# A mixture of experts in float32: the second layer in four column chunks, the spread by row groups, and each further pass in a condition of its own

## The reference

```python
logits = xt @ w_router + b_router                 # 256 x 32
top_v, top_e = lax.top_k(logits, 4)
weights = jax.nn.softmax(top_v, axis=-1)
# for each expert e and its tokens:
hcat = x @ w1[e] + b1[e]                          # 1024 -> 2048
x_glu = minimum(hcat[:, ::2], 7.0)
x_lin = clip(hcat[:, 1::2], -7.0, 7.0)
act = x_glu * sigmoid(1.702 * x_glu) * (x_lin + 1.0)
y = act @ w2[e] + b2[e]                           # 1024 -> 1024
# out[token] = sum over its 4 experts of weight * y
```

## Time and profile before

| | before |
|---|---|
| median of 3 runs | 2322.46 us (2321.23 to 2323.91) |
| the profiled execution, its own time | 2310.58 us |
| its span, first to last instruction | 2308.8 us |
| busy PE, DVE, ACT, POOL | 80%, 35%, 22%, 3% |
| moved by DMA | 713.56 MB |
| the first mixture's experts, in the span | from 427.6 to about 1460 us |

### The profile page before, as it was taken

How to read it: one execution, slowest core, us unless ns; L and a number is a source line. 1 busy time by engine, 2 the same in 40 slices (tenths; PEclk the granted TensorE clock), 3 DMA queues, 4 the chain that set the end, 5 groups by cost and what they waited for, 6 DMA issues and landing times. The chain is left out here.

```text
span 2308.8 us, 28283 instructions
## 1 busy us (share of the span) xinstructions
PE 1839.7 (80%) x11518; PEld 837.9 (36%) x11518; DVE 811.2 (35%) x1618; ACT 496.6 (22%) x1005; POOL 76.8 (3%) x96
## 2 busy tenths in 40 slices
PE   7899998888989988789977788689968656555555
PEld 3655545433333333333333333354524422222221
DVE  2224332333433334433344334687682300000001
ACT  2032301222222133332333333321301200000000
POOL 0000000000000000000000000291000000000000
PEclk9999999899999999999999999799989777777778
DMA  8745268498797699999999999432126399999996
GB/s 287 268 146 181 93 215 310 176 398 329 328 388 318 278 424 408 422 424 376 406 423 423 423 417 420 143 117 103 40 73 236 122 426 428 428 427 427 425 424 260
DMA packets 113956, 713.56 MB, mean 309 GB/s; under 512 B 16703, under 2 KB 21006, under 8 KB 68654
## 3 DMA queue, kind: packets, MB, share of 16 engines
q1 hardware_dynamic: 105344, 704.98, 75.3%
q10 hardware_dynamic: 8398, 5.47, 0.8%
HBM read 709.35 MB, written 1.07 MB: 308 GB/s over the span
## 5 line engine op out<-in xcount | busy, mean ns | idle before, releaser
L779 PE MATMUL ps<-ring,ar 128*32 128x512 f32 x3072 | 374.5, 627 | 50.2 <-DMA ring<-in_w 21.7
L434 PE MATMUL ps<-ar 128*128 128x128 f32 (+5 forms) x1750 | 357.9, 361 | 41.9 <-PEq L691 13.4
L441 PE MATMUL ps<-ring,ar 128*32 128x512 f32 x1536 | 211.5, 713 | 192.1 <-DMA ring<-in_w_up 81.0
L434 PEld LDWEIGHTS ps<-ar 128*128 128x128 f32 (+2 forms) x1750 | 235.9, 201 | 165.8 <-issue 111.1
L434 PE MATMUL ps<-ring,ar 128*128 128x512 f32 (+2 forms) x624 | 262.9, 581 | 18.0 <-DVE ar L1855 9.9
L779 PEld LDWEIGHTS ps<-ring,ar 128*32 128x32 f32 x3072 | 99.8, 113 | 318.9 <-issue 275.8
L1610 DVE TENSOR_SCALAR ar<-ps 128x256 f32<-128x256 f32 x128 | 54.4, 425 | 432.2 <-PE ps L779 425.5
L790 PE MATMUL ps<-ring,ar 128*32 128x512 f32 x1536 | 175.2, 595 | 21.7 <-ACT ar L2207 21.7
L441 PEld LDWEIGHTS ps<-ring,ar 128*32 128x32 f32 x1536 | 60.6, 129 | 337.0 <-issue 336.1
L434 PEld LDWEIGHTS ps<-ring,ar 128*128 128x128 f32 x624 | 119.2, 193 | 156.4 <-issue 135.6
L538 PE MATMUL ps<-ring,ar 128*128 128x512 f32 x384 | 172.4, 598 | 3.4 <-ACT ar L2038 3.4
(11 more groups left out here) (393 smaller groups left out, 1290.5 us busy)
## 6 DMA issues: line engine op xcount, KB each, us to landing
ring<-in_w SPq DMA_DIRECT2D x192, 2048.0 KB, 18.4
ring<-in_w_gate SPq DMA_DIRECT2D x32, 2048.0 KB, 17.8
ring<-in_w_up SPq DMA_DIRECT2D x32, 2048.0 KB, 16.8
ring<-in_w_down SPq DMA_DIRECT2D x32, 2048.0 KB, 16.3
ring<-in_w_in SPq DMA_DIRECT2D x21, 2048.0 KB, 8.1
ring<-in_w_ada SPq DMA_DIRECT2D x12, 2048.0 KB, 8.6
ring<-in_w_out SPq DMA_DIRECT2D x4, 2048.0 KB, 8.1
ring<-in_w_branch SPq DMA_DIRECT2D x6, 1024.0 KB, 5.0
```

The lines of the kernel that those rows point to most:

```text
L434: ins = self.t.e.matmul(o, l, r, start=(i == 0), stop=(i == len(pairs) - 1))
L441: ins = self.t.e.matmul(b[32 * i:32 * i + 32, :], l, r, start=(k == 0), stop=(k == len(steps) - 1))
L779: ins = e.matmul(b[32 * s:32 * s + 32, :], HG[:, 2 * c + r, 32 * n:32 * n + 32], W[:, r, HALF(s)], start=False, stop=(c == 3 and r == 1))
```

## The change

Layer two: each pass has 32 matmuls of 256 columns instead of 16 of 512. Column group `c` holds result columns 256c to 256c+255 and sums the whole contraction. ACT evicts a pass in one instruction of 128x256. Spread: the stationary operand is now one row group (32 rows) of `SWT1`, the moving one 256 columns of `YG1`; 8 matmuls for each pass go side by side through four row groups into four banks. DVE then does four additions of 128x512 for each expert, in all cases. It stands between the halves of layer one. Conditions: each further pass has its own, in the order 3, 2, 1; the last of them counts on semaphores of its own (`s_px`, `s_py`, `s_ps`), and the Else no longer waits for `s_pe`. The count of expert `u + 1` is loaded once, in the second half of layer one. `turn_act(0)` moves into the middle of the next gather, and `turn_act(1)` runs always, before layer two. DVE does the spread's additions ahead of pass 0. `AT1` and `SB1` have one buffer instead of two.

```diff
+    def only(t, count, limit, body):
+        n, met = t.n, dict(t.met)
+        with t.e.If(count > limit):
+            body()
+        assert t.n == n
+        t.met = met
+
+    def either(t, x, count, limit, body):
+        n, m, met = t.n, x.n, dict(t.met)
+        with t.e.If(count > limit):
+            body()
+        assert t.n == n
+        t.met = met
+        with t.e.Else():
+            if m > 0:
+                t.e.wait_ge(x.sem, m)
+            t.e.nop().then_inc(x.sem, x.n - m)
...
+        def gather1(u, count, between):
+            pe["sw1", u, 0] = t(weights_turned(u, 0, (4,)))
+            rows_in(u, 0, (5,))
+            between()
+            only(t, count, 64, lambda: weights_turned(u, 2, (6,)))
+            rows_in(u, 1, (4,))
...
+        def spread1(u, count):
+            b = [w.claim("sp", u, c, lane=(SP1[c],)) for c in range(4)]
+            def rows(n, tb, first, last):
+                for c in range(4):
+                    r = slice(32 * c, 32 * c + 32)
+                    ins = e.matmul(b[c][:, 256 * tb:256 * tb + 256], SWT1[u % 2][r, n, TB(tb)], YG1[r, n, :],
+                                   start=first, stop=last)
+                return ins
+            t.wait_ge(s_act, act["yg", u, 0])
+            with e.If(count > 32):
+                for tb in range(2):
+                    t.wait_ge(s_act, act["yg", u, 1])
+                    rows(1, tb, True, False)
+                    def later():
+                        t.wait_ge(s_act, act["yg", u, 3])
+                        rows(2, tb, False, False)
+                        rows(3, tb, False, False)
+                    only(t, count, 64, later)
+                    ins = rows(0, tb, False, True)
+                z(ins)
+            with e.Else():
+                for tb in range(2):
+                    ins = rows(0, tb, True, True)
+                ins.then_inc(s_ps, z.n - n)
...
-            def layer2(b, n, arrive):
+            def layer2(b, n, arrive, first):
...
-                    for h in range(2):
-                        for r in range(2):
-                            ins = e.matmul(b[64 * h + 32 * r:64 * h + 32 * r + 32, :],
-                                           AT_[:, 2 * s + r, 32 * n:32 * n + 32], W[:, s % 2, r, HALF(h)],
-                                           start=(s == 0), stop=(s == 3))
+                    for r in range(2):
+                        for c in range(4):
+                            ins = e.matmul(b[32 * c:32 * c + 32, 0:256], AT1[:, 2 * s + r, 32 * n:32 * n + 32],
+                                           W[:, s % 2, r, 256 * c:256 * c + 256], start=(s == 0 and r == 0),
+                                           stop=(s == 3 and r == 1))
...
+                only(t, count, 96, lambda: further(3))
+                only(t, count, 64, lambda: further(2))
+                either(t, x, count, 32, lambda: x(further(1)))
...
+                if half == 0 and u > 0:
+                    spread1(u - 1, counts[u - 1])
...
-            if u > 0:
-                spread(t, w, 1, u - 1, TL1)
-            turn_act(0, (0,))
             if u + 1 < NE:
-                gather(t, w, 1, u + 1, TL1)
+                gather1(u + 1, counts[u + 1], turn_first)
+            else:
+                turn_first()
+            turn_act(1, (1,), (5,))
...
+            only(t, count, 64, lambda: turn_act(2, (2, 3), (6,)))
...
+            either(t, x, count, 32, second)
+            px["l2", u] = x.n
+            only(t, count, 96, fourth)
+            either(t, y, count, 64, third)
...
 vector_moe1
+            if u > 0:
+                vector_spread1(v, u - 1)
             for n in range(4):
-                M = TM[n % 2]
+                M = TM1[n % 2]
...
-                if n == 0 and u > 0:
-                    vector_spread(v, 1, u - 1)
...
 scalar_moe1
         for u in range(NE):
             sigmoid(u, 0)
+                weights_turned(u + 1, 0)
+            sigmoid(u, 1)
+                rows_in(u + 1, 0)
+            turned_act(u, 0, (0,))
+                weights_turned(u + 1, 2)
+                rows_in(u + 1, 1)
+            turned_act(u, 1, (1,))
+            sigmoid(u, 2)
+            sigmoid(u, 3)
+            evict(u, 0)
+            turned_act(u, 2, (2, 3))
             for n in (1, 2, 3):
+                evict(u, n)
```

More of the change, by code:

```diff
@@ L761, in tensor_moe1, with weights_turned, rows_in @@
         t.wait_ge(s_b1, 16)
-        gather(t, w, 1, 0, TL1)
+        x, y, z = Queue(e, s_px), Queue(e, s_py), Queue(e, s_ps)
+        def weights_turned(u, n0, lane):
+            b = w.claim("sw1", u, n0, lane=lane)
+            t.wait_ge(s_dve, dve["sel", 1, u])
+            for n in range(2):
+                for tb in range(2):
+                    ins = e.transpose(b[:, TB(2 * n + tb)], SWB1[:, tb, TB(n0 + n)], ident)
+            return ins
+        def rows_in(u, h, lane):
+            t.wait_ge(s_act, act["rows", 1])
+            b = w.claim("hg", 1, u, h, lane=lane)
+            for k in range(4):
+                m = w.sums(b[:, TB(k)], [(XNV[:, tb, TB(4 * h + k)], SB1[:, tb, :]) for tb in range(2)])
+                pe["hg", 1, u, h, k] = m
@@ L799, in turn_act @@
                     for r in range(2):
[L800 to L804, removed]
-            for half in range(2):
-                done = t(layer1(bl[0], 0, half, True))
-                def further():
-                    if half == 0:
[L810 to L817, removed]
+                        ins = e.transpose(b[:, TB(2 * i + r)], AC1[:, n, TB(r)], ident)
@@ L831, in second, with fourth @@
                 t.wait_ge(s_act, act["at", u, 1])
[L832 to L836, removed]
+                x(layer2(w.claim("l2", u, 1, lane=(1,)), 1, False, first_third))
+            def fourth():
                 t.wait_ge(s_act, act["at", u, 2])
-                with e.If(count > 96):
-                    layer2(b[1], 3, False)
-                pe["l2x", u] = t(layer2(b[0], 2, False))
@@ L845, in tensor_moe1 @@
+            py["l2", u] = y.n
             for g in range(2):
                 w.free("w2", u, g)
-        spread(t, w, 1, NE - 1, TL1)
+                px["free", "w2", u, g], py["free", "w2", u, g] = x.n, y.n
+        spread1(NE - 1, counts[NE - 1])
     def tensor_dense2(t, w):
@@ L1520, in vector_ranks, with vector_select1 @@
         dve["flag", m] = v(v.own.tensor_copy(F[:, 0:1].bitcast(I32), F[:, 1:2]))
-    def vector_select(v, m, u):
+    def vector_select1(v, u):
+        if u > 0:
+            v.wait_ge(s_pe, pe["hg", 1, u - 1, 1, 3])
+        v(v.own.tensor_tensor(SB1, bc(iota, 1, [128, 2, 128]), RK[:, :, u:u + 1].to_broadcast([128, 2, 128]),
+                              ALU.is_equal))
+        for tb in range(2):
+            four = bc(SB1[:, tb].rearrange("p (n s) -> p n s", n=4), 2, [128, 4, 4, 32])
+            k = v(v.own.tensor_scalar(SWB1[:, tb].rearrange("p (n c s) -> p n c s", n=4, c=4), four,
+                                      CMB[:, tb, u:u + 1], None, ALU.mult))
+        dve["sel", 1, u] = k
@@ L1523, in vector_select @@
+    def vector_select(v, u):
         if u > 1:
-            v.wait_ge(s_pe, pe["hg", m, u - 2, 1, 3])
+            v.wait_ge(s_pe, pe["hg", 2, u - 2, 1, 3])
         if u > 0:
[L1526 to L1557, removed]
+            v.wait_ge(s_pe, pe["swt", 2, u - 1])
@@ new lines, in vector_select, with vector_spread1 @@
+        four = [z[:, :, 4 * u:4 * u + 4].unsqueeze(3).to_broadcast([128, 2, 4, 32]) for z in (RK, CMB)]
+        S = SB[u % 2].rearrange("p b (x s) -> p b x s", x=4)
+        v(v.own.tensor_tensor(S, iota[:, 0:32].unsqueeze(1).unsqueeze(1).to_broadcast([128, 2, 4, 32]), four[0],
+                              ALU.is_equal))
+        k = v(v.own.tensor_tensor(SWB[:, 0].rearrange("p b (x s) -> p b x s", x=4), S, four[1], ALU.mult))
+        dve["sel", 2, u] = k
+    def vector_spread1(v, u):
+        v.wait_ge(s_ps, psp["sp", u])
+        for c in range(4):
+            o = YV[:, :, 256 * c:256 * c + 256]
+            v(v.own.tensor_tensor(o, ps("sp", u, c).rearrange("p (b n) -> p b n", b=2), o, ALU.add))
+            read["sp", u, c] = v.mark()
+        dve["y", 1, u] = v.n
@@ L1559, in vector_moe1, with vector_spread @@
+    def vector_spread(v, u):
+        for tb in range(2):
+            for h in range(2):
+                v.wait_ge(s_pe, pe["sp", 2, u, tb, h])
+                o = YV[:, tb, HALF(h)]
+                v(v.own.tensor_tensor(o, ps("sp", 2, u, tb, h)[:, :], o, ALU.add))
+                read["sp", 2, u, tb, h] = v.mark()
     def vector_moe1(v):
@@ L2177, in evict @@
+        def evict(u, n):
+            if n == 0:
+                s.wait_ge(s_pe, pe["l2", u, 0])
+            elif n == 1:
+                s.wait_ge(s_px, px["l2", u])
+            else:
+                s.wait_ge(s_py, py["l2", u])
+            if u > 0:
+                s.wait_ge(s_ps, psp["sp", u - 1])
             s.wait_ge(s_dve, dve["ac", u, n])
[L2178 to L2180 removed]
```

(1 more changed line is left out.)

241 lines of the change are left out of this document (137 added, 104 removed).

## The result

| | before | after |
|---|---|---|
| median of 4 runs each | 2321.85 us | 2362.21 us (2360.08 to 2368.11) |
| ratio, 95% interval | 1 | 1.0174 [1.0159, 1.019] |
| span of the profiled execution | 2308.8 us | 2361.5 us |
| mean granted clock of PE | 0.916 | 0.882 |
| experts 0 to 9 (A) | 367.5 us | 367.0 us |

The changed kernel is 40 us slower by the medians; I had forecast 60 us less. In them A took as long as before, the tail became 5 us shorter, and B lost 59 us.

The account below looks back on a forecast made before the run. PE was taken to bound experts 0 to 9, DMA the rest except for pockets. Terms of -42.3, -10 and -7.5 us made -59.8, so 2262 us on the runs' median; likeliest case 2250 to 2274, whole range 2246 to 2297.

Parts of the forecast that it names:

- the tail: From the last weights landing to the last addition, 14.85 us before: only pass 0 awaited, 7.3 us left, -7.5 us.
- B: Mixture after expert 9: bound by DMA except for pockets worth 15.4 us, of which 10 us were to come back.
- PE's backlog of 3.6 us of matmuls ahead of each jump: At the conditions: matmuls queued ahead of a jump, named as the argument against jumps each costing over 2 us.
- the 14.5 us saved at an expert's start: Bias matmuls opening an expert in A: of 15.7 us of waits for banks and end gaps, 14.5 us would go.
- rivals 1 and 2: Conditions are dear: in part, 1 to 3 us per expert in A, 2278 to 2302 us (0.20); or fully, slower (0.05).
- rival 2: Three jumps per expert in A each stand open over 2 us: 66 us lost against 60 gained, 2328 us; chance 0.05.
- My own sign of being wrong: Profile after: "PEq" or "issue" waits on PE in A coming to more than 10 us.
- A's gain of 42.3 us: Experts 0 to 9: sum of PE's savings and added costs, -42.3 us, all counted in full.
- Spread: Spread in A: 20 passes at 1.17 us, 23.4 us instead of 45.2, saving 21.8 us.
- Rival 3: Layer two in chunks costs 5.6 us a pass, not 3.9: +34 us in A, 2296 us; chance 0.07.
- Waits for ACT before further passes, 13.0 us: Layer two in A: turning activations a pass earlier hides ACT's eviction under matmuls, saving 13.0 us.
- Rival 4: DMA bounds the whole mixture and PE's time doesn't matter: only the tail gains, 2315 us; chance 0.05.

Follow-up runs that it names:

- f1: The kernel before without pass 3 on PE in both layers, cap 96 tokens, 208 instructions fewer per expert: 2306.97 us, ratio 0.9945.
- e1: The kernel before with three never-run copies of layer two's pass 3, 192 instructions per expert: 2395.61 us, ratio 1.0306.
- f3: The changed kernel with each weight DMA of the first mixture bringing 16 of 128 partitions from expert 2 on: 2207.55 us, single execution.
- e2: The changed kernel without pass 3 on PE (layer one, layer two, spread), cap 96 tokens: 2272.56 us, ratio 0.9775 against the changed kernel's 1.0174.
- f2: The kernel before with each weight DMA of the first mixture bringing 16 of 128 partitions from expert 2 on: 2278.8 us, single execution.
- g3: The kernel before without pass 3 on PE, plus 192 never-run instructions per expert in layer two's third pass: 2328.47 us, ratio 1.0031.

## Why the prediction was wrong

The failed step is the sentence "PE's backlog of 3.6 us of matmuls ahead of each jump speaks against it", with the 14.5 us saved at an expert's start that rest on it. I named the mechanism as rivals 1 and 2 and gave the slower one 0.05; rival 2's price was three jumps of 2.2 us each in A. Measured were 22.1 us in four gaps at the start of an expert, 5.5 us each beyond the backlog, and 40.3 us in all. My own sign of being wrong was 10 us of such waits in A. The waits that the 14.5 us stood for did go, but for 0.7 us; what my sum put at nothing are the waits for code, and they eat A's gain of 42.3 us by themselves. B then adds 59 us more of loss.

My evidence was one-sided. The 0.18 us gaps in A came from a kernel whose code per expert the fetch could just keep up with. That they stood at 3.25 and 2.05 us in B was the sign that it was at its edge: f1, with 208 instructions fewer per expert, has only 0.2 us gaps, and e1, with 192 more, has 4.4 us on average. The change adds 48 packets x 256 / 32 = 384 instructions net per expert. I had written "twice the instructions" and counted the cost by conditions and not by pages. The Trainium skill's rule that I cited with the rivals (Runtime: NRT & Kernel Launch, Instruction fetch mechanics), that a taken branch to a page not at hand waits for its fetch, agrees with the 24 gaps at an expert's start. Two things only the runs show: the skipped pages are fetched all the same (e1's 24 packets), and the wait at an expert's start is 4.7 us beside full weight transfers and 1.8 us beside light ones (after, f3).

Point by point:

- Spread: forecast 1.17 us a pass, 1.18 measured. Layer two: 3.9 forecast, 3.67 measured. Rival 3 falls.
- Waits for ACT before further passes, 13.0 us: gone. What came instead is 0.8 us for DVE before `turn_act(2)`, four times in A; I had it at nothing.
- Sum in A without the waits for code: 40.8 us saved (36.0 like for like), 42.3 forecast. The terms are right in kind; that they agree so closely is in part luck, since layer two cost 5.4 us less than its term (72.6 us for 78.0), and layer one with its bias matmuls 9.8 us more at the lower clock, for which there was no term. e2, which still has some of the waits, shows 32 us.
- B: "the rest of B goes by DMA" was half true. f2 shows that with light transfers the old kernel still needs 603 us there, so it had 39 us of slack for 22 experts, 1.8 us each, and my -10 us left the waits for code out. In the changed kernel 20 gaps at an expert's start come to 89.6 us, and the other two rows shown to 37.4 us more. PE stands still 62.5 us longer than before and is busy 3 us less: the work saved was made up for by layer one, 25 us longer, and its bias matmuls, 18 us longer, at the lower clock. B became 59 us longer, where I had -10.
- Tail: -5.3 us from the last matmul of layer one on, forecast -7.5 us from the last weights on. `turn_act` waits for DVE there since no gather stands between, which I had left out (timeline of the changed kernel, last expert):

```profile
1492.84 4.21 PE L853 MATMUL ps<-ring,ar 128*32 128x512 f32 x32
...
1499.32 0.41 PE L878 MATMUL ps<-ar 128*128 128x128 f32 x2 [2.27 <-DVE ar L1724]
...
1501.39 0.69 PE L878 MATMUL ps<-ar 128*128 128x128 f32 x2 [1.66 <-DVE ar L1724]
...
1511.50 2.87 DVE L1646 TENSOR_TENSOR ar<-ps,ar 128x512 f32<-128x512 f32 x4 [4.75 <-PE ps L809]
```

Layer one ends at 1497.05 and the last addition at 1514.37, 17.3 us later; before these were 1437.30 and 1459.95.

- Rival 4 (DMA bounds all) falls with A's 334 GB/s and with e2, f1 and f3.

What stays open: how many pages PE holds ahead, what sets the half of the waits that light transfers leave, and why g3 is slower than the kernel before. That one dose of 24 packets costs 21 us and the next 72 us fits with slack being used up, as the waits for weights show (52.6 us in f1, 10.4 in g3; 21.7 before, none in e1), but it wasn't tested by itself. The lower clock behind the gaps wasn't tested apart from them either.

## What to carry to other kernels

Where conditions skip much code, count instructions per round as a resource of their own: round time against pages, with the packets of the instruction queue on the page as the measure, before asking what the executed part costs. A change that halves the width of matmuls doubles their code, also in the branches that are not taken. If small waits at conditions already grow where DMA is full, the fetch is at its edge, and taking out never-run branches can be worth more than the edit itself: here 90 us for a pass that no expert needed, some 8 us of it work that ran in the spread.

## What the runs showed of the hardware that was not expected

192 instructions per expert that never ran cost 72 us (ratio 1.0306), in either of two places. They were fetched all the same: 24 packets of 16.4 KB. At an expert's start the wait for code behind the jumps depended on the data transfers beside it, 4.7 against 1.8 us on average; at the spread it didn't. Seven more conditions for each of 32 experts cost some 5 us together, 0.10 us each of PE's time at their place.
